# Two more merge gates computed as fills inside the RWKV part of a two-block hybrid mixer

## Chip, cores and metric

The kernel runs on one core of a Trainium2 chip. The metric is the device time of one execution in microseconds; lower is better. For a kernel the median of several runs counts.

## What is computed

The input is 256 tokens of width 2048 (x) and 256 context tokens (ctx). The first block is a hybrid mixer with four branches (a convolution, a state-space scan "SSD", a Fourier branch and an RWKV-7 scan), whose outputs are merged by gates, and then an MLP; a second block follows. The part that matters is the merge, for 256 tokens and D = 2048:

```python
def gated_merge(gate_pre, branches, w_o):
    b, l, _ = gate_pre.shape
    gates = jax.nn.sigmoid(gate_pre).reshape(b, l, N_BRANCH, D_MODEL)
    m = gates[:, :, 0] * branches[0]
    for i in range(1, N_BRANCH):
        m = m + gates[:, :, i] * branches[i]
    return m @ w_o
```

`gate_pre` is a slice of `u = h @ w_in`: 4 x 2048 columns, each a sum over 2048. It depends on h alone, so it can be computed as soon as h is there, long before the branches are done. The RWKV branch is a recurrence over tokens for 8 heads, forwards and backwards, first over the context (state only), then over the tokens (state and output).

## The kernel before

**Units and slots.** Weights come in units of 1024 KB (128 input features on the partitions, 16 such tiles kt, 128 output columns) through a ring of four slots. SP issues every fetch: the fetch of unit u waits until unit u - 4 is used up (`w_used`). Queues run in order, so whatever SP waits for holds up all that stands behind it.

**Gates.** The merge goes over 8 pairs of output tiles (p = 0..7), with four gates each (b = 0..3), one per branch: 32 gates. A gate takes two units (o = 0, 1) and fills one PSUM bank of 128 x 512.
- Gates b = 0 and 2 of every pair, 16 in all (`FILLS`), are computed early, as *fills*: `fill(pe, n)` (line 953) issues the next n plain fp32 matmuls of 128x128 by 128x256 (line 966) of one running list of 32 per gate, in places chosen by hand, where TensorE would wait. The matmul is recorded as two instructions. The first three gates are fills of the SSD part, the other 13 of the RWKV part.
- ACT turns a finished bank into a gate with a sigmoid (`fill_gates`, line 975, recorded at line 980), at one place in each round: `fills_by(r)` (line 971) works out from `FILL_PREP`, `FILL_ROUND` and `FILL_EARLY` how many gates are complete there. SP then stores it in DRAM (`keep_gate`, line 984, recorded at 986). In `RwScan.sync` the fetch of gate k is followed by the storing of gate k - 2.
- Gates b = 1 and 3 are computed in the merge itself, in `Merge.tensor`, with weights and h split in high and low parts: three fp32r products per tile (lines 2067 to 2069), 96 a gate. ACT rounds each unit (`round_unit`, line 2310), DVE takes the difference (`rest_unit`, line 2315), three and two units ahead.

**Preparation of the RWKV part** (`RwIn`, lines 1229 to 1386). TensorE projects 14 tiles (line 535). ACT copies each into a padded buffer (1290, 1294), DVE shifts and mixes them (1350 to 1354). Then TensorE turns the values (line 1246, "turned values", four banks), multiplies the learning-rate part (1251, waits for `al_ready`, which DVE raises at line 1358 after the last shift), the output gate (1258), makes 12 fills, the sums for the key norm (1265), 12 fills, and the bonus sums (1272). ACT makes sigmoids (1308), copies (1311), squares (1316) and roots (1323). DVE ends with four reciprocals (1375) and the bonus (1382), and raises `prep_ready` (1386).

**The rounds** (`RwScan`, from line 1493). Eight rounds: for each of four head pairs j first the context (half = 1), then the tokens (half = 0). Before them TensorE computes the first decays (`decays(0)`, line 1512) and 24 fills. A round on TensorE: 7 fills; products of the scaled keys (1531), after DVE's line 1806; turned tiles (1572, 1573), 4 fills; five levels of the triangular inverse (1542, 1556) with fills between; turned left side (1600); *masked products* (`products`, 1531: one pair of banks in a context round, three in a token round), which DVE masks at line 1846; the next round's decays (1512); inverse right side (1616), after the mask, copied by ACT at line 1768; 6 or 3 fills; the inverse applied (1542, `tav`), after that copy; 3 fills; the state updates (1636 to 1643); in a token round also 1656 and then the *output* `y_in` (1669, 1672); 3 fills; the chunk states (1695) and in a token round 1709. In ACT's queue between the levels and line 1768 stand the decay gates of the next round (table load and two sigmoids, 1724) and the kept gates (980). There are 47 fills in a context round and 44 in a token round.

**The merge** (`Merge`, from line 2047). SP fetches, for each pair, the four units, then the branch weights `bo_u[p]` (2304 KB, one buffer, after the products of pair p - 1), then, after the sums of pair p - 1 (`merged`), the two kept gates (256 KB each). TensorE: gate, gate, then 36 matmuls of branch outputs by branch weights (line 2086). DVE: four times a unit's difference and one column of the second block's modulation (rows of 1024 KB, fetched by POOL, 389), then the products with the gates (2162 to 2168).

## Time and profile before

| | us |
|---|---|
| median of 3 runs (lowest to highest) | 3455.66 (3454.62 to 3462.45) |
| the profiled execution's own time | 3459.0 |
| its span in the profile | 3457.3 |
| TensorE busy / DVE / ACT | 3283.2 / 2166.8 / 1183.7 |
| preparation of the RWKV part after its projections, from and to | 711 to 765 |
| eight rounds, from and to | 765 to 1164 |
| merge, from and to | 1172 to about 1482 |

The profile is of one execution. TensorE's matmuls overlap, and their ends are modelled: the time that a row of equal instructions takes is read from start to start. A timeline row gives start, duration, engine, line, instruction, operands and count, and in brackets the idle time before it with what ended it.

### The profile page before, as it was taken

Reading aid. Unit: us, or ns where it says so; the run is one execution under the profiler, and the core shown is the slowest. Engines: PE = TensorE matmul, PEld = TensorE weight load, DVE = VectorE, ACT = ScalarE, POOL = GpSimd, SP = SyncE. Lnnn points to the kernel's source line nnn. Section 1 sums busy time; section 2 is a strip of 40 time slices with the busy share of each in tenths; the row PEclk is TensorE's granted clock in tenths of the full one; section 3 lists DMA queues with packets and bytes.
Section 4 is the critical chain, followed back from the end, with each engine's and each line's share of the span. In section 5 each row is a group of like instructions: output and inputs, shape, how many; then the busy total and the mean of one; then the engine's idle time right before and its main releaser. Section 6 shows DMA issues by size and latency. Waiting matters only on the chain.

```text
span 3457.3 us, 57768 instructions
## 1 busy us (share of the span) xinstructions
PE 3283.2 (95%) x23026; PEld 2687.1 (78%) x23026; DVE 2166.8 (63%) x3283; ACT 1183.7 (34%) x1550; POOL 188.6 (5%) x298
## 2 busy tenths in 40 slices
PE   6899989989998899998999999998999999999998
PEld 3674676457777799987888888886888788888887
DVE  2185654663333565667777777787656767667767
ACT  1212021022222321234434343444544543444344
POOL 0000000111222100000000000000000000000000
PEclk9999999999999999999999999999999999999999
DMA  9864624722112477754676767673444556656654
GB/s 364 327 230 170 264 105 158 292 92 84 71 44 84 190 309 307 292 185 158 246 263 235 272 229 282 231 268 122 158 153 176 172 193 234 235 187 229 233 177 151
DMA packets 99280, 706.33 MB, mean 204 GB/s; under 512 B 11008, under 2 KB 11008, under 8 KB 17920
## 3 DMA queue, kind: packets, MB, share of 16 engines
q1 hardware_dynamic: 74880, 523.27, 41.5%
q0 software_dynamic: 23184, 169.88, 13.3%
q10 hardware_dynamic: 1008, 10.23, 0.7%
q8 instruction: 152, 2.49, 0.3%
q14 instruction: 56, 0.46, 0.0%
HBM read 697.05 MB, written 6.29 MB: 203 GB/s over the span
## 4 chain that ended last, share of the span: by engine, by line
PE 76%; DVE 9%; issue 6%; ACT 4%; DMA 3%; DVEq 0%; ACTq 0%; SPq 0%; POOLq 0%
PE ps L2352 25%; PE ps L2351 13%; PE ps L535 10%; PE ps L966 6%; PE ps L2086 3%; ACT rows_parts L2310 3%; PE ps L355 2%; PE ps L1542 2%; PE ps L2348 2%; PE ps L2068 2%; PE ps L2067 2%; PE ps L2069 2%; PE ps L1556 1%; DVE work L2196 1%; DMA ring<-in_conv_u 1%
## 5 line engine op out<-in xcount | busy, mean ns | idle before, releaser
L2352 PE MATMUL ps<-hT_parts,rows_parts 128*128 128x512 f32 x3210 | 1129.8, 394 | 0.0
L2351 PE MATMUL ps<-hT_parts,ring_parts 128*128 128x256 f32 x3210 | 900.7, 281 | 2.0 <-DVE hT_parts L2324 2.0
L2315 DVE TENSOR_TENSOR ring_parts<-ring,rows_parts 128x2048 fp32r<-128x2048 f32 (+1 forms) x340 | 769.6, 2264 | 208.6 <-ACT rows_parts L2310 207.2
L2310 ACT ACTIVATE rows_parts<-ring 128x2048 fp32r<-128x2048 f32 (+1 forms) x340 | 643.8, 1895 | 414.9 <-DMA ring<-in_mlp_u 167.6
L2352 PEld LDWEIGHTS ps<-hT_parts,rows_parts 128*128 128x128 f32 x3210 | 603.5, 188 | 125.6
L2351 PEld LDWEIGHTS ps<-hT_parts,ring_parts 128*128 128x128 f32 x3210 | 608.0, 189 | 12.9 <-DVE hT_parts L2324 3.2
L2352 PE MATMUL ps<-work_parts,rows_parts 128*128 128x512 f32 x1616 | 573.3, 396 | 0.0
L2351 PE MATMUL ps<-work_parts,ring_parts 128*128 128x256 f32 x1616 | 453.1, 280 | 4.6 <-DVE work_parts L2540 4.6
L535 PE MATMUL ps<-hT,ring 128*128 128x512 f32 (+1 forms) x1088 | 374.2, 505 | 7.4 <-ACT work L1294 4.3
L2352 PEld LDWEIGHTS ps<-work_parts,rows_parts 128*128 128x128 f32 x1616 | 303.6, 188 | 68.2
L535 PEld LDWEIGHTS ps<-hT,ring 128*128 128x128 f32 x1088 | 206.0, 190 | 173.8 <-issue 162.1
L2351 PEld LDWEIGHTS ps<-work_parts,ring_parts 128*128 128x128 f32 x1616 | 304.3, 188 | 11.0 <-DVE work_parts L2540 5.9
L966 PE MATMUL ps<-hT,ring 128*128 128x256 f32 x1024 | 271.5, 403 | 3.1 <-DVEq L1386 3.1
L2395 ACT ACTIVATE work<-ps 128x256 f32<-128x256 f32 (+1 forms) x220 | 83.2, 378 | 465.0 <-PE ps L2352 457.2
L2400 DVE TENSOR_TENSOR work<-work,ps 128x256 f32<-128x256 f32 (+1 forms) x220 | 92.1, 418 | 197.1 <-ACT work L2395 176.4
L966 PEld LDWEIGHTS ps<-hT,ring 128*128 128x128 f32 x1024 | 187.2, 195 | 33.4 <-DVEq L1386 3.5
L389 DVE CUSTOM_DVE_ANT_0 rows<-rows 128x2048 f32<-128x2048 f32 x64 | 146.4, 2288 | 37.7 <-DMA rows<-in_mod_r 37.6
L2196 DVE CUSTOM_DVE_ANT_0 work<-work,K 128x2048 f32<-128x2048 f32 x64 | 146.2, 2285 | 4.1 <-DMA work<-in_ada_r 4.0
L2069 PE MATMUL ps<-hT_parts,ring_parts 128*128 128x256 f32 x512 | 145.1, 283 | 0.0
L2086 PE MATMUL ps<-work 128*128 128x256 f32 x576 | 125.6, 379 | 0.0
L1826 DVE TENSOR_TENSOR work<-work,ps 128x64 f32<-128x64 f32 x288 | 42.2, 213 | 133.1 <-PE ps L1556 132.0
L2086 PEld LDWEIGHTS ps<-work 128*128 128x128 f32 x576 | 108.8, 190 | 14.5
(444 smaller groups left out, 3784.3 us busy)
## 6 DMA issues: line engine op xcount, KB each, us to landing
ring<-in_mlp_u SPq DMA_DIRECT2D x128, 1024.0 KB, 4.9
ring<-in_ffn_u SPq DMA_DIRECT2D x88, 1024.0 KB, 4.8
rows<-in_mod_r POOLq DMA_DIRECT2D x64, 1024.0 KB, 5.2
ring<-in_gate_u SPq DMA_DIRECT2D x64, 1024.0 KB, 6.7
work<-in_ada_r POOLq DMA_DIRECT2D x64, 1024.0 KB, 5.1
ring<-in_in_u SPq DMA_DIRECT2D x36, 1024.0 KB, 4.8
ring<-in_mod_u SPq DMA_DIRECT2D x32, 1024.0 KB, 7.7
rows<-in_ada_r POOLq DMA_DIRECT2D x32, 1024.0 KB, 7.6
```

What stands on the lines that cost most here:

```text
L389: dve.tensor_tensor_reduce(rows_buf[:, j, :], rows_buf[:, j, :], conditioning, 1.0, 0.0, ALU.mult, ALU.add, g_acc[:, j:j + 1]).then_inc(ro ...
L535: mm = pe.matmul(outs[o], wtile(u + o, kt), rhs(kt), start=kt == 0, stop=kt == KT - 1)
L966: mm = pe.matmul(ps[:, use_fill[k][0], o * T:(o + 1) * T], wtile(u, kt), main_rhs(kt), start=kt == 0, stop=kt == KT - 1)
L2069: mm = pe.matmul(out, low, h_high[:, kt, :], start=False, stop=kt == KT - 1)
L2086: mm = pe.matmul(ps[:, 3 + b, o * T:(o + 1) * T], bo_buf[:, at + kt, o * P:(o + 1) * P], src[:, kt, :], start=kt == 0, stop=kt == kts - 1)
L2196: dve.tensor_tensor_reduce(late_row, late_row, c2_row, 1.0, 0.0, ALU.mult, ALU.add, acc).then_inc(late_free, 1)
L2310: act.activation(unit_high(u)[:, 0:size], slot(u)[:, 0:size], ACT.Copy).then_inc(hi_done, 1)
L2315: dve.tensor_tensor(ring_parts[:, u % SLOTS, 0:size], slot(u)[:, 0:size], unit_high(u)[:, 0:size].bitcast(F32), ALU.subtract)\
L2351: pe.matmul(ps[:, b, low_half], low, top(kt), start=False, stop=False)
L2352: mm = pe.matmul(ps[:, b, :], high, both(kt), start=False, stop=kt == kts - 1)
L2395: act.activation(dst, ps[:, b:b + 1, half], ACT.Copy).then_inc(half_out, 1)
L2400: dve.tensor_tensor(dst, dst, ps[:, b:b + 1, half], ALU.add).then_inc(bk.free[b], 1)
```

## The change

Gate 1 of pair 3 and gate 1 of pair 5 become fills too, and are kept in DRAM like the others: 18 fills instead of 16 (15 in the RWKV part), 14 gates in the merge instead of 16. The 64 more fill matmuls stand: 12 before the turned values, 8 more after the first decays (24 becomes 32), 3 after the first masked products in all rounds, 2 before the inverse is applied and 3 before the output in token rounds. ACT reads gate 3 before the first decay exponentials instead of in round 0, and the number of gates read in each round follows the new counts. In the merge, pairs 3 and 5 have one computed gate and three kept ones; DVE makes the same four columns a pair; SP fetches each pair's units up to four past its first one. The host lays the weight columns out in the new order.

```diff
--- before.py
+++ after.py
@@ -58,6 +58,9 @@
 UNIT = KT * P
 PARTS2 = (16, 16, 12)
 BO_K = CT + ST + FT + RT
+MORE_KEPT = ((3, 1), (5, 1))
+KEPT_GATES = [(p, b) for p in range(KT // 2) for b in (0, 2)] + list(MORE_KEPT)
+MERGE_GATES = [(p, b) for p in range(KT // 2) for b in (1, 3) if (p, b) not in MORE_KEPT]
 
 
 
@@ -932,8 +935,9 @@
         ssq = w(S0 + 5632, ST * T, a=ST)
 
         PAIRS2 = KT // 2
-        FILLS, SSD_FILLS = 2 * PAIRS2, 3
-        FILL_PREP, FILL_ROUND, FILL_EARLY = 48, 44, 31
+        FILLS, SSD_FILLS = len(KEPT_GATES), 3
+        FILL_PREP, FILL_HALF, FILL_FULL, FILL_EARLY = 68, 50, 52, 31
+        FILL_FIRST = 36
         seg_ssd_fill = segment(2 * SSD_FILLS)
         use_fill = [bk.take(k) for k in range(SSD_FILLS)]
         fill_gate, fill_stored = sem("fill_gate"), [sem(f"fill_stored{n}") for n in range(2)]
@@ -970,7 +974,10 @@
 
         def fills_by(r):
 
-            return min(FILLS - 1, SSD_FILLS + (FILL_PREP + FILL_ROUND * r + FILL_EARLY) // (2 * KT)) if r >= 0 else SSD_FILLS
+            if r < 0:
+                return SSD_FILLS + FILL_FIRST // (2 * KT)
+            before = FILL_PREP + r // 2 * (FILL_HALF + FILL_FULL) + r % 2 * FILL_HALF
+            return min(FILLS - 1, SSD_FILLS + (before + FILL_EARLY) // (2 * KT))
 
         def fill_gates(act, first, last):
             for k in range(first, last):
@@ -1239,6 +1246,7 @@
                     both = n >= 2
                     outs = [ps[:, 0, :], ps[:, 1, :]] if both else pair(n % 2)
                     gemm_pair(pe, seg_rw + 2 * n, both_rhs if both else main_rhs, outs, rw_uses[n])
+                fill(pe, 12)
                 for a in range(NT):
                     pe.wait_ge(shifted, 3 * RT)
                     acquire(pe, use_vt[a])
@@ -1513,7 +1521,7 @@
                                   lora_t[d * LORA:(d + 1) * LORA, half * T:(half + 1) * T], start=True, stop=True).then_inc(bk.full[use[0]], 1)
 
                 decays(0)
-                fill(pe, 24)
+                fill(pe, 32)
                 pe.wait_ge(prep_ready, 1)
                 for r, (j, half) in enumerate(ROUNDS):
                     u = rounds[r]
@@ -1604,6 +1612,8 @@
                             pe.wait_ge(rsem["r_ready"][d], j + 1)
                     for n, (left, right) in enumerate(((3, 0),) if half else ((3, 0), (1, 4), (3, 4))):
                         products([u["nt"][h][n] for h in range(2)], left, right)
+                        if n == 0:
+                            fill(pe, 3)
                     if r + 1 < len(ROUNDS):
                         decays(r + 1)
                     for h in range(2):
@@ -1616,6 +1626,8 @@
                                 mm = pe.matmul(ps[across(odd), use[0], blk(i)], BIG[h][0][rows, blk(i)], v_of(h, a, rows), start=True, stop=True)
                         mm.then_inc(bk.full[use[0]], 1)
                     fill(pe, 6 if half else 3)
+                    if not half:
+                        fill(pe, 2)
                     evacuated(pe, u["at"])
                     for h in range(2):
                         evacuated(pe, u["nv"][h])
@@ -1657,6 +1669,7 @@
                                                start=True, stop=True)
                                 if i == len(UNITS) - 1 and h == 1:
                                     mm.then_inc(bk.full[u["rh"][odd][0]], 1)
+                        fill(pe, 3)
                         use = u["y_in"]
                         acquire(pe, use)
                         for a in range(TT):
@@ -1730,6 +1743,7 @@
                         act.activation(dec_mem(2, d), dec_mem(1, d), ACT.Exp, scale=DECAY).then_inc(rsem["dec_exp"][d], 1)
 
                 decay_gates(0)
+                fill_gates(act, SSD_FILLS, fills_by(-1))
                 decay_exps(0)
                 act.wait_ge(prep_ready, 1)
                 for r, (j, half) in enumerate(ROUNDS):
@@ -1983,8 +1997,8 @@
                         .then_inc(yt_aff, 1)
 
 
-        seg_merge = segment(4 * PAIRS2)
-        MERGE_END = seg_merge + 4 * PAIRS2
+        seg_merge = segment(2 * len(MERGE_GATES))
+        MERGE_END = seg_merge + 2 * len(MERGE_GATES)
         MERGE_ROWS = 4 * PAIRS2
         bo_buf = w(W0, BO_K * 2 * P, k=BO_K)
         gates = w(W0 + BO_K * 2 * P, 8 * T, b=4)
@@ -1992,7 +2006,7 @@
         m_all = w(M0, KT * T, a=KT)
         H0 = M0 + KT * T
         assert H0 + UNIT <= WORK
-        use_gate = [bk.take(b, PAIRS2) for b in range(2)]
+        use_gate = [bk.take(n, sum(b == g for _, b in MERGE_GATES)) for n, g in enumerate((1, 3))]
         use_bo = [bk.take(3 + b, PAIRS2) for b in range(4)]
         bo_ready = sem("bo_ready")
         merged = sem("merged")
@@ -2000,14 +2014,24 @@
         h_hi, h_split, x_again = sem("h_hi"), sem("h_split"), sem("x_again")
 
         GATED = (1, 3)
-        KEPT = (0, 2)
         kept_in = sem("kept_in")
 
+        def gated(p):
+
+            return [n for n, b in enumerate(GATED) if (p, b) in MERGE_GATES]
+
+        def kept(p):
+
+            return [b for b in range(4) if (p, b) in KEPT_GATES]
+
         def merge_unit(p, n, o=0):
-            return seg_merge + 4 * p + 2 * n + o
+            return seg_merge + 2 * MERGE_GATES.index((p, GATED[n])) + o
+
+        def merge_units(p):
+            return [merge_unit(p, n, o) for n in gated(p) for o in range(2)]
 
         def gate_use(p, n):
-            return n, use_gate[n][1] + p
+            return n, use_gate[n][1] + sum((q, GATED[n]) in MERGE_GATES for q in range(p))
 
         def unit_high(u):
 
@@ -2025,13 +2049,13 @@
 
         class Merge:
             def sync(sp):
+                fetched = seg_merge
                 for p in range(PAIRS2):
-                    for n in range(2):
-                        for o in range(2):
-                            u = merge_unit(p, n, o)
-                            sp.wait_ge(w_used, u - SLOTS + 1)
-                            sp.dma_start(slot(u), gate_u[2 * FILLS + u - seg_merge]).then_inc(w_ready[u % SLOTS], 16)
-                        if p == 0 and n == 0:
+                    for u in range(fetched, min(merge_unit(p, gated(p)[0]) + SLOTS, MERGE_END)):
+                        sp.wait_ge(w_used, u - SLOTS + 1)
+                        sp.dma_start(slot(u), gate_u[2 * FILLS + u - seg_merge]).then_inc(w_ready[u % SLOTS], 16)
+                        fetched = u + 1
+                        if u == seg_merge + 1:
                             keep_gate(sp, FILLS - 2)
                     if p == 0:
                         keep_gate(sp, FILLS - 1)
@@ -2046,13 +2070,13 @@
                     else:
                         for n in range(2):
                             sp.wait_ge(fill_stored[n], 8 * FILLS)
-                    for n, b in enumerate(KEPT):
-                        sp.dma_start(gates[:, b, :], gate_kept[2 * p + n]).then_inc(kept_in, 16)
+                    for b in kept(p):
+                        sp.dma_start(gates[:, b, :], gate_kept[KEPT_GATES.index((p, b))]).then_inc(kept_in, 16)
 
             def tensor(pe, own):
                 fill(pe, 2 * FILLS * KT - fills_read[0])
                 for p in range(PAIRS2):
-                    for n in range(2):
+                    for n in gated(p):
                         use = gate_use(p, n)
                         acquire(pe, use)
                         for o in range(2):
@@ -2100,7 +2124,8 @@
                 fill_gates(act, FILLS - 1, FILLS)
                 for p in range(PAIRS2):
                     act.wait_ge(merged, p)
-                    for n, b in enumerate(GATED):
+                    for n in gated(p):
+                        b = GATED[n]
                         for o in range(2):
                             u = merge_unit(p, n, o)
                             if u == seg_merge + 1:
@@ -2138,18 +2163,20 @@
                 RwOut.vector_scaled(dve, own)
                 m_pairs = m_all.rearrange("p (j o) t -> p j o t", o=2)
                 for p in range(PAIRS2):
-                    for n in range(4):
-                        u = seg_merge + 4 * p + n + AHEAD_DVE
+                    units = merge_units(p)
+                    for n, u in enumerate(units):
+                        u += AHEAD_DVE
                         if u == seg_merge + 1 + AHEAD_ACT:
                             RwOut.vector_out(dve, own)
                         rest_unit(dve, u)
-                        at = 4 * p + n
-                        for i in (at,) if p else () if n < 2 else (2 * n - 4, 2 * n - 3):
+                        late = n if p else n - 2
+                        each = 4 // (len(units) if p else 2)
+                        for i in range(4 * p + late * each, 4 * p + (late + 1) * each) if late >= 0 else ():
                             if i == 0:
                                 dve.wait_ge(c2_moved, 1)
                             column(dve, adaT, vec("ada_b"), c2_row, ADA0 + i, i)
-                    dve.wait_ge(kept_in, 32 * p + 32)
-                    for n in range(2):
+                    dve.wait_ge(kept_in, 16 * sum(len(kept(q)) for q in range(p + 1)))
+                    for n in gated(p):
                         evacuated(dve, gate_use(p, n))
                     if p == PAIRS2 - 1:
                         unit_done(dve, MERGE_END - 1)
@@ -3468,7 +3495,7 @@
 
     bo = np.concatenate([i[k][0] for k in ("conv_out", "ssd_out", "fourier_out", "rwkv_out")], 0)
     gates = w_in[:, gt:].reshape(D, 4, KT // 2, 2 * P)
-    gates = np.concatenate([gates[:, n::2].transpose(0, 2, 1, 3).reshape(D, -1) for n in range(2)], 1)
+    gates = np.concatenate([gates[:, b, p] for p, b in KEPT_GATES + MERGE_GATES], 1)
     ffn = np.stack([i["w_ffn_gate_2"][0].reshape(D, KF2, P), i["w_ffn_up_2"][0].reshape(D, KF2, P)], 2).reshape(D, -1)
 
     up, down = i["mlp_up"][0], i["mlp_down"][0]
```

## Rows read from the trace of the kernel before

**Rows 1.** The page: span, and busy time of each engine

```profile
span 3457.3 us, 57768 instructions
...
PE 3283.2 (95%) x23026; PEld 2687.1 (78%) x23026; DVE 2166.8 (63%) x3283; ACT 1183.7 (34%) x1550; POOL 188.6 (5%) x298
```

**Rows 2.** Stretches: length, busy PE, PEld, DVE, ACT, POOL; granted clock, DMA, GB/s

```profile
712.00:772.00 60.00, 51.18 (x275) 37.19 (x273) 40.37 (x55) 22.60 (x43) 5.20 (x7) 0.86 0.15 53
...
823.00:878.00 55.00, 49.03 (x1021) 39.47 (x1013) 19.77 (x80) 13.50 (x31) 10.52 (x15) 0.94 0.13 45
...
1237.00:1275.00 38.00, 38.00 (x264) 36.19 (x263) 25.17 (x27) 10.27 (x8) 2.64 (x5) 1.00 0.80 306
...
718.30:725.40 7.10, 7.10 (x8) 2.49 (x8) 5.12 (x10) 2.06 (x3) 0.00 (x0) 0.50 0.01 2
```

**Rows 3.** Timeline of TensorE in the preparation of the RWKV part

```profile
718.30 7.19 PE L1251 MATMUL ps<-work 64*128 64x512 f32 x8 [5.41 <-DVEq L1358]
725.42 3.78 PE L1258 MATMUL ps<-work 128*128 128x256 f32 x8
728.99 5.90 PE L966 MATMUL ps<-hT,ring 128*128 128x256 f32 x24
734.73 3.79 PE L1265 MATMUL ps<-work,K 128*128 128x512 f32 x8
738.35 5.34 PE L966 MATMUL ps<-hT,ring 128*128 128x256 f32 x24
743.53 1.89 PE L1272 MATMUL ps<-work,K 128*128 128x256 f32 x8
...
759.75 4.98 PE L966 MATMUL ps<-hT,ring 128*128 128x256 f32 x14 [3.14 <-DVEq L1386]
```

**Rows 4.** Timeline of DVE in the same stretch

```profile
739.37 3.35 DVE L1375 RECIPROCAL work<-work 128x512 f32<-128x512 f32 x1 [10.20 <-ACT work L1323]
...
764.47 0.42 DVE L1806 TENSOR_TENSOR work<-rows,work 128x256 f32<-128x256 f32 x1
```

**Rows 5.** Waits, 772 to 1164: who waited for whom, total us, times, longest

```profile
PE ps L1531 <- DVE work L1846: 5.3, 4, 1.3
PE ps L1669 <- issue: 5.3, 3, 3.4
...
PE ps L1616 <- DVE work L1846: 4.3, 4, 1.1
...
PE ps L1542 <- issue: 2.9, 3, 1.5
PE ps L1672 <- issue: 2.8, 1, 2.8
```

**Rows 6.** Timeline of TensorE around the output of the first two token rounds

```profile
853.45 0.26 PE L1672 MATMUL ps<-work 64*64 64x64 f32 x1 [2.79 <-issue]
...
855.88 2.93 PE L966 MATMUL ps<-hT,ring 128*128 128x256 f32 x6
858.74 0.69 PE L1695 MATMUL ps<-work 64*64 64x64 f32 x8
...
953.89 0.22 PE L1672 MATMUL ps<-work 64*64 64x64 f32 x1
...
955.33 1.56 PE L966 MATMUL ps<-hT,ring 128*128 128x256 f32 x6
956.82 0.45 PE L1695 MATMUL ps<-work 64*64 64x64 f32 x8
```

**Rows 7.** Timeline of ACT in round 0

```profile
795.91 0.66 ACT L1768 ACTIVATE work<-ps 128x256 f32<-128x256 f32 x2
```

**Rows 8.** The chain that ended last, in order of time: start, us, what

```profile
1236.28 15.54 PE ps L2086 x72
1274.69 15.54 PE ps L2086 x72
```

**Rows 9.** The eight fetches of branch weights, their time to landing

```profile
DMA to landing us min/median/max: 8.4/9.0/10.5
```

**Rows 10.** DMA issues from 772 to 1164: KB each, median us to landing

```profile
ring<-in_gate_u SPq DMA_DIRECT2D x23, 1024.0 KB, 5.8
```

## The prediction

> **What bounds the kernel now.** I read the page first [rows 1]: TensorE is busy 3283.2 of 3457.3 us, so a change counts by what it adds to or takes from TensorE's own stream, and by the 174 us in which that stream stands still. Then the busy time by stretches [rows 2]: in a merge pair (1237 to 1275) TensorE is busy the whole 38.00 us at clock 1.00, DVE 25.17, ACT 10.27, DMA at 0.80. In the preparation (712 to 772) and in a closing round (823 to 878) TensorE has 9 and 6 us of holes and a mean granted clock of 0.86 and 0.94. Then TensorE's timeline there [rows 3, 5, 6] and the engines it waits for [rows 4, 7]. "Issue" in a row is idle time for which the profile shows no semaphore.
>
> **Removed.** Two gates (branch 1 of pairs 3 and 5) leave the merge. The products with the branch outputs (L2086) start at 1236.28 and again at 1274.69, and take 15.54 [rows 8]. So a pair lasts 38.41 us, of which 38.41 - 15.54 = 22.87 are its two gates: 11.43 each. TensorE has no hole there [rows 2], so two gates give 2 x 11.43 = **-22.9 us**. Their four weight units, roundings (ACT) and differences (DVE) go too, off the path.
>
> **Added.** The same two gates as plain fp32 fills: 64 matmuls, each two instructions at L966. At full clock 24 instructions go from 738.35 to 743.53 [rows 3], 216 ns each, so one fill is 0.432 us and 64 are 27.6 us. At full price the change would lose 4.8. All hangs on where they stand.
>
> *Preparation, 12 fills before the turned values (5.2 us) and 8 more after the first decays (3.5 us).* TensorE turns the values at 711 and then stands 5.41 us until VectorE has shifted the last tile (L1358) at 718.30 [rows 3]. That release hangs on DVE and ACT, not on TensorE, so 5.2 us fit in front; the values are then turned from about 716.3 to 718.1, with nothing late. After that hole the trace shows granted clock 0.50, that is 1.2 GHz instead of 2.4, from 718.3 to 725.4 [rows 2]: L1251 takes 7.12 us to the start of L1258 [rows 3]. Without the hole the engine goes on at 2.4 GHz: L1251 3.56 (-3.6), L1258 3.57 to the start of the fills, now 1.7 by 8 x 216 ns (-1.8), and the 24 fill instructions 5.74 instead of 5.18 (-0.6). Sum -6.0. It passes on, since DVE's reciprocals (L1375) at 739.37 waited 10.20 us for ACT's roots [rows 4], and these for TensorE's L1265. I expect ACT's sigmoids at L1308 to keep up with products that come twice as fast; rival 2 is the case that they don't. The 0.1 us that ACT's copies of the values come later I take off: **-5.9**. From L1375 on DVE sets the pace until prep_ready at 759.7; the 8 fills (3.5) stand in the 3.14 us hole at 759.75 [rows 3], whose wait I expect at about 0, as TensorE itself is 5.9 earlier too. ACT's extra sigmoid, of fill 3, lies in its wait for DVE's first sums. Round 0 still starts when DVE's L1806 is through (764.47 + 0.42 [rows 4]), 5.9 earlier. The fills after 759.75 took 4.98 for 14 instructions at the low clock; running faster they only wait for L1806.
>
> *Masked products, 3 fills (1.3 us) in each of 8 rounds.* In the four context rounds TensorE waits 4.3 us in all at L1616, in the four others 5.3 at L1531 [rows 5], each time for DVE's masking. The fills come ahead of the next round's decays, so in a context round ACT's table load, decay gates and kept gates start 1.3 us later and the copies of L1768, at 795.91 + 0.38 [rows 7], come at about 797.6 where TensorE begins L1542 at about that time today. That is 0.4 instead of 0.2 beyond cover in three of them. Sum: 4 x 1.3 - 4.3 + 0.45 = +1.35; in the others 5.2 - 5.3 = 0.
>
> *Before the turned inverse times values (L1542), 2 fills in four rounds (3.45 us).* The holes there are 2.9 in three rounds, the longest 1.5 [rows 5], so 0.7 + 0.7 + 0.86 are covered and the last round has none: **+1.15**.
>
> *Before the output (L1669), 3 fills in four rounds (5.2 us).* Here TensorE stands 5.3 + 2.8 = 8.1 us in four holes, 3.4 and 2.8 and two of about 1, marked "issue" [rows 5]. They fall at different matmuls of the same line, so no semaphore of that line makes them. They come behind the longest run of 64-column products without a fill in it (L1636 to L1672). I take them for instructions that arrive late; the trace does not prove this. If so, 1.3 us of slow matmuls ahead of it shortens each hole by up to 1.3: 1.3 + 1.3 + 0.9 + 1.0 = -4.5. After the 2.79 us hole the rest runs at the low clock: 853.45 to 858.74 is 5.29 us, where after a hole of 1 us 953.89 to 956.82 is 2.93, and six fill instructions last 2.93 instead of 1.56 [rows 6]. A hole of 1.5 us is followed by full clock elsewhere (L1531's 1.33), so that loss of 2.4 goes. The 3.4 hole shrinks to 2.1, between 1.5 and 2.79; both ends are equally near, and I take the loss, some 3.0, as kept. Together 5.2 - 4.5 - 2.4 = **-1.7**. Bounds: +5.2 (no hole shrinks) and -8.3 (all holes and both clock losses gone: 5.2 - 8.1 - 5.4).
> The Trainium skill, page "Runtime: NRT & Kernel Launch", section "Instruction fetch mechanics", says that instructions are refilled in 16 KiB blocks and that this is mostly hidden behind the rate at which instructions issue. By that rule the holes are no late instructions and the fills cost their +5.2; the row of 8.1 us speaks against it, without settling it.
>
> *Queues.* Each fetch on SP stands behind the storing of an earlier gate. The tightest is now fill 13: it waits for gate 10, read by ACT in round 4, and is needed at the 320th fill of this part, the last but two of that round. In times of round 0 that is SP at about 797 and TensorE at about 807, for a landing of 5.8 us [rows 10]: 4 us to spare, price 0. In the merge, the branch weights of pairs 3 and 5 must land in the 11.43 us of one gate instead of 22.87; they take 8.4 to 10.5 [rows 9]. One more gate of 256 KB beside them, by 2304 KB in 9.0 us, is 1.0 us at worst: 11.5, nothing to 0.1 late. DVE is busy 25.17 us of 38 in a pair of today [rows 2], and loses two of its four differences. Price 0, bound +5 each.
>
> **Sum.** -22.9 - 5.9 + 1.35 + 0 + 1.15 - 1.7 = **-28.0 us**. The profiled execution took 3459.0 (span 3457.3) and goes to 3431.0; it lies 3.3 above the median of the three runs, 3455.66, which goes to **3427.7**.
>
> **Rivals.**
> 1. *The output's holes stay*: +5.2 in place of -1.7, the sum -21.1: 3434.6. For it: the holes' cause is unproven. Against: they sit where instructions are shortest. The page named above would give just this. 0.15.
> 2. *The preparation gains nothing*: the hole is filled but the copies of the values come late, or the clock stays low, so +0.3 for the 8 fills in place of -5.9: 3433.9. For it: ACT does sigmoids and copies one behind the other. Against: clock 0.50 begins exactly behind the hole. 0.10.
> 3. *The merge becomes bound by transfers* in its two short pairs: two weight units, the branch weights, three gates and four rows of the modulation matrix are 9216 KB or 9.4 MB, in 27 us 350 GB/s, above the 306 of [rows 2]. At 306 a pair needs 31 us: +4 each, 3435.5. 0.06.
> 4. *Nothing is covered*: -22.9 + 27.6 = +4.8, 3460.4, which is no change. Against: 29 us of holes stand in [rows 3, 5], before any low clock is counted. 0.04.
> 5. *Slower: a weight unit arrives late in each round*, because its fetch is queued behind a gate's store that waits for ACT, which the new fills push back. A hole of 2.8 us and its clock loss of 2.4 are 5.2, in 8 rounds 41.8: -28.0 + 41.8 = +13.8, 3469.5. It decides once a landing takes over 10 us. Against: 5.8. 0.03.
> That the gates are not moved at all I leave out: the lists are 18 and 14 gates by count.
> The forecast itself has 0.62.
>
> **The numbers.** About 0.3%, 10.4 us, is what a measurement can tell. Faster: the forecast and rivals 1 to 3, 0.93; same: rival 4 and a mixture, 0.04; slower 0.03. Low end: all holes and both clock losses gone, 6.6 below, with 2 for the rest: 3419. High end: rivals 1 and 2 together, 3440.8: 3441.
>
> **What would show it.** TensorE's hole before L1251 under 0.5 us and L1251 at 427 ns a start at clock 1.00; prep_ready about 6 us earlier; no wait at L1616's and L1531's places; the holes before and in the output under 1.6 us but one; pairs 3 and 5 of the merge at 27 us with TensorE unbroken; the merge starting 5 us sooner than before (-5.9 - 1.7 + 1.35 + 1.15). Wrong if the merge starts no earlier, or if L2086 waits in pairs 3 and 5.

## Result, and the profile after

| | before | after |
|---|---|---|
| median (lowest to highest) | 3456.89 (3454.62 to 3462.45), 4 runs | 3425.14 (3423.72 to 3434.82), 4 runs |
| ratio, with its 95% interval | | 0.9911 [0.9892, 0.993] |
| the profiled execution's own time | 3459.0 | 3434.82 |

The change takes 31.75 us, 0.9%. Forecast were 28.0 and a time of 3427.7: the direction, the range and the size are right. Two parts of the sum are not, and their errors cancel in large part. The profiles were cut into five stages behind a common start; the stages' lengths are differences of start times in the timeline.

| stage, us | before | before again | after | after again |
|---|---|---|---|---|
| start of the learning-rate product (1251, now 1259) | 718.30 | 717.73 | 728.08 | 725.11 |
| from there to round 0 | 46.70 | 46.18 | 40.91 | 40.91 |
| round 0 to the first gate product of the merge | 406.95 | 400.72 | 410.51 | 408.82 |
| first gate product to first branch product | 25.85 | 25.36 | 25.55 | 24.86 |
| first to last branch product | 284.1 | 284.1 | 261.2 | 261.2 |
| last branch product to the end | 1975.41 | 1976.40 | 1966.85 | 1966.09 |

"Again" are two more executions, from the experiments below. The first row holds work that the change doesn't touch; over all profiles of this study it lies between 716.4 and 728.1 in no order. It is what scatters, so single executions can't be compared by their ends, but by their stages they can.

The page of the kernel after (answers to rows 1):

```profile
span 3433.1 us, 57659 instructions
...
PE 3284.7 (96%) x22962; PEld 2689.7 (78%) x22962; DVE 2160.1 (63%) x3279; ACT 1177.9 (34%) x1546; POOL 188.6 (5%) x298
```

TensorE is as busy as before (3283.2 in [rows 1]), in a span 24.2 us shorter: the same work with fewer holes. DVE and ACT have four instructions of work fewer each. That small number becomes important below.

TensorE's timeline in the preparation, after (answers to rows 3):

```profile
720.77 5.34 PE L970 MATMUL ps<-hT,ring 128*128 128x256 f32 x24
725.95 1.91 PE L1254 MATMUL ps<-K,work 128*128 128x128 f32 x16
728.08 3.70 PE L1259 MATMUL ps<-work 64*128 64x512 f32 x8 [0.22 <-DVEq L1366]
731.71 1.99 PE L1266 MATMUL ps<-work 128*128 128x256 f32 x8
733.54 5.34 PE L970 MATMUL ps<-hT,ring 128*128 128x256 f32 x24
738.72 3.79 PE L1273 MATMUL ps<-work,K 128*128 128x512 f32 x8
...
749.98 17.10 PE L970 MATMUL ps<-hT,ring 128*128 128x256 f32 x78
768.99 1.16 PE L1539 MATMUL ps<-work 64*64 64x64 f32 x64 [1.91 <-issue]
```

The hole of 5.41 us is down to 0.22, and the product behind it takes 3.63 us (728.08 to 731.71) instead of 7.12. The windows of the same trace, with the columns of rows 2, give the clock:

```profile
728.10:735.00 6.90, 6.90 (x23) 4.33 (x24) 5.75 (x11) 5.16 (x10) 0.00 (x0) 1.00 0.01 2
...
1281.93:1308.83 26.90, 26.90 (x170) 25.04 (x169) 18.69 (x19) 4.39 (x4) 1.58 (x3) 1.00 0.70 268
...
1308.83:1347.24 38.41, 38.41 (x266) 36.55 (x265) 23.49 (x25) 8.46 (x6) 2.11 (x4) 1.00 0.89 353
```

The first: granted clock 1.00 where it was 0.50. The second is pair 3, with one computed gate: TensorE is busy through all 26.90 us. The third is pair 4: the queues move 353 GB/s, with TensorE as busy. The chain that ended last has the branch products:

```profile
1281.93 15.54 PE ps L2110 x72
...
1308.83 15.54 PE ps L2110 x72
...
1347.24 15.54 PE ps L2110 x72
...
1374.29 15.54 PE ps L2110 x72
```

26.90, 38.41, 27.05: two pairs lost 11.5 and 11.4 us, and 22.9 together.

TensorE's waits from 766 to 1185, after (answers to rows 5; line 1682 is the old 1669, 1539 the old 1531, 1550 the old 1542, 1668 the old 1656, 1652 the old 1640):

```profile
PE ps L2091 <- DVE hT_parts L2160: 7.5, 1, 7.5
PE ps L1682 <- issue: 3.4, 2, 1.9
PE ps L1539 <- issue: 3.3, 4, 1.9
...
PE ps L1668 <- DVE work L1871: 1.9, 1, 1.9
PE ps L1652 <- issue: 1.5, 1, 1.5
...
PE ps L1550 <- ACT work L1782: 0.6, 3, 0.2
PE ps L1550 <- issue: 0.5, 1, 0.5
```

The waits for DVE's masks (5.3 and 4.3 in [rows 5]) are gone. The holes in the runs of 64-column products, 8.1 before, are 6.8 now (3.4 + 1.9 + 1.5), at other lines. The 1.9 is put down to VectorE, but TensorE's two semaphore instructions there begin only at 856.16 and take 0.05 us each, so they found nothing to wait for: it is counted with the others. And the wait of 7.5 at the head of the merge, which was there before as well, still is.

Last, the part behind the merge, which the edit doesn't touch and which the prediction didn't name, is 8.6 us shorter. VectorE's rows for the line at the head of the MLP loop, before and then after (the loop makes four turns, each a quarter of the hidden width):

```profile
L2400 DVE TENSOR_TENSOR work<-work,ps x220: 407/420/424, 1490.2 to 3375.3; 128x256 f32<-128x256 f32 x94, 128x256 f32 x16
...
  issue: 20.4, 3
```

```profile
L2427 DVE TENSOR_TENSOR work<-work,ps x220: 409/420/424, 1473.9 to 3351.0; 128x256 f32<-128x256 f32 x94, 128x256 f32 x16
...
  issue: 11.9, 3
```

The same instruction stands still three times, at the three turns of the loop, for no semaphore: 20.4 us in all before, 11.9 after. The difference, 8.5, is the stage's.

### The profile page after: what moved, and what is told of

It is laid out like the page before. It is cut to its first block, busy times and chain, and to the rows that moved or that the text cites. A ratio compares the mean times of both kernels' runs of the same rounds, so it can differ in the third digit from the quotient of the medians.

```text
span 3433.1 us, 57659 instructions
## 1 busy us (share of the span) xinstructions
PE 3284.7 (96%) x22962; PEld 2689.7 (78%) x22962; DVE 2160.1 (63%) x3279; ACT 1177.9 (34%) x1546; POOL 188.6 (5%) x298
## 4 chain that ended last, share of the span: by engine, by line
PE 81%; DVE 7%; issue 5%; ACT 4%; DMA 3%; DVEq 0%; ACTq 0%; POOLq 0%; SPq 0%
PE ps L2379 27%; PE ps L2378 14%; PE ps L538 10%; PE ps L970 6%; PE ps L2110 4%; PE ps L358 2%; ACT rows_parts L2337 2%; PE ps L2375 2%; PE ps L1550 2%; PE ps L2092 2%; PE ps L2091 2%; PE ps L2093 2%; PE ps L1564 1%; DMA ring<-in_conv_u 1%; DVE work L2223 1%
## 5 line engine op out<-in xcount | busy, mean ns | idle before, releaser
L2378 PE MATMUL ps<-hT_parts,ring_parts 128*128 128x256 f32 x3210 | 900.9, 281 | 1.6 <-DVE hT_parts L2351 1.6
L538 PEld LDWEIGHTS ps<-hT,ring 128*128 128x128 f32 x1088 | 206.0, 190 | 173.8 <-issue 162.1
L970 PE MATMUL ps<-hT,ring 128*128 128x256 f32 x1152 | 297.2, 396 | 0.0
L970 PEld LDWEIGHTS ps<-hT,ring 128*128 128x128 f32 x1152 | 207.1, 191 | 32.5 <-issue 2.7
L2093 PE MATMUL ps<-hT_parts,ring_parts 128*128 128x256 f32 x448 | 127.0, 283 | 0.0
```

Source lines behind the costliest of these rows:

```text
L538: mm = pe.matmul(outs[o], wtile(u + o, kt), rhs(kt), start=kt == 0, stop=kt == KT - 1)
L970: mm = pe.matmul(ps[:, use_fill[k][0], o * T:(o + 1) * T], wtile(u, kt), main_rhs(kt), start=kt == 0, stop=kt == KT - 1)
L2093: mm = pe.matmul(out, low, h_high[:, kt, :], start=False, stop=kt == KT - 1)
L2378: pe.matmul(ps[:, b, low_half], low, top(kt), start=False, stop=False)
```

## Experiments

Three questions stood open. Is the gain of the preparation due to the fills ahead of the turned values? Do fills ahead of the output shorten its holes, or do the holes go by where the instructions lie (theory P of the expectations)? And where do the 9 us behind the merge come from: VectorE's code lying four instructions earlier (theory A1), or ACT's?

### How much of a profile is chance

The two kernels unchanged, once more: before_again and after_again.

> The kernel before once more, for a second trace. Between the end of the merge and the end of the MLP the changed kernel's trace is 8.9 us shorter than that of before, although nothing there was edited: VectorE stands 6.3, 6.9 and 7.3 us at the turn of the MLP's loop before, 4.6, under 3.5 and 4.3 after. Theory A (the place of the code in memory sets the stall): this second trace shows 6 to 7 us again at each turn. Theory B (chance of one execution, for instance what the transfers do at that moment): the stalls come out anywhere between 3 and 7.5. Both: the holes before the output in the token rounds (2.8, 0.8, 3.4, 1.1) repeat within 0.3 if they are fixed by the code, and scatter if by chance.

> The changed kernel once more, against before in three rounds. Its profiled execution had a start 9.8 us longer than that of before, in stages not edited; without it its own time would be 3425, as in the other runs. Expected: ratio 0.991, some 31 us less. By Theory A 25 of these come from the edited stages and 6 to 9 from the loop of the MLP in every run; by Theory B only about 25 to 28 us as a mean, and the MLP's stalls are other than 4.6, under 3.5, 4.3.

after_again took 3426.42, before beside it 3460.44 (7 runs, 3448.45 to 3465.4): ratio 0.9913 [0.9882, 0.9944]. Stages as in the table. VectorE's stops at the turns of the loop repeat: 7.0, 7.1 and 7.0 us in before_again (6.3, 6.9, 7.3 before), 4.1, 4.5 and 3.3 in after_again. So do before's holes around the output: 2.82, 0.50, 3.17 and 1.10 against 2.79, 0.78, 3.44 and 1.10. Both speak for the code's place. Rounds 1 and 5 of the kernel before took 56.29 and 57.86 us in the first profile, 53.49 and 54.78 now, with holes that are nearly as long (3.2 and 2.8). TensorE's row behind the hole in round 1 of before_again, and the window around it, columns as in rows 2:

```profile
852.44 0.21 PE L1672 MATMUL ps<-work 64*64 64x64 f32 x1 [2.82 <-issue]
```

```profile
851.00:860.00 9.00, 6.80 (x112) 5.22 (x111) 1.42 (x6) 3.00 (x6) 0.00 (x0) 1.00 0.01 2
```

Clock 1.00 behind a hole of 2.82 us, where the first profile had half of it for 5.29 us behind one of 2.79 [rows 6]. In the two padded versions of before, below, rounds 1 and 5 took 56.1 to 56.3 us, so the loss comes in three of four executions and is no fixed part of the kernel. It isn't bound to long holes either: in after_dve_pad4, below, whose TensorE code is that of after, the clock is at 0.50 for 3.4 us behind holes of 1.91 and 1.94 us that left it at 1.00 in after.

### The first 12 fills behind the hole again (first_fills_late)

```diff
-                fill(pe, 12)
                 for a in range(NT):
                     pe.wait_ge(shifted, 3 * RT)
...
-                fill(pe, 32)
+                fill(pe, 44)
                 pe.wait_ge(prep_ready, 1)
```

> The changed kernel with the 12 fills taken from before the turned values and put behind the first decays (44 fills there instead of 32). My theory: the hole of 5.4 us before L1259 comes back, the clock falls to 0.50 behind it and costs 6.0 us, and the 5.2 us of fills are no longer covered: TensorE then reaches round 0 by 19.0 us of fills and 3.0 more after the decays, so that round 0 starts about 9 us later than in the changed kernel (50 instead of 40.9 us after L1259's start). Time +9, about 3434. Rival (the fills in the hole keep no clock up, VectorE's chain sets the time anyway): the start of round 0 moves by at most 3 us.

TensorE's timeline of first_fills_late:

```profile
723.15 7.19 PE L1258 MATMUL ps<-work 64*128 64x512 f32 x8 [5.40 <-DVEq L1365]
730.27 3.78 PE L1265 MATMUL ps<-work 128*128 128x256 f32 x8
```

The hole is back, and so is the product at half clock. Round 0 begins 50.01 us after the learning-rate product, against 40.91: +9.1. The key sums (line 1272) begin at 739.70, 16.55 us behind that product instead of 10.64, so the low clock costs 5.9; the 12 fills cost 5.2, less the 1.9 us hole ahead of round 0, which is gone. The time is 3431.67 (3429.96 to 3439.85) against 3426.42 (3422.59 to 3431.44), +5.3 with ranges that overlap; ratio 0.9927 [0.9899, 0.9956]. The stage shows the effect, the medians only its sign. The forecast for this place is shown by removal.

### Output fills moved into the wait at the merge (output_fills_to_merge)

```diff
-        FILL_PREP, FILL_HALF, FILL_FULL, FILL_EARLY = 68, 50, 52, 31
+        FILL_PREP, FILL_HALF, FILL_FULL, FILL_EARLY = 68, 50, 49, 31
...
-                        fill(pe, 3)
                         use = u["y_in"]
...
             def scalar(act, own):
+                fill_gates(act, fills_by(len(ROUNDS) - 1), FILLS - 1)
```

The 12 fills then stand at the end of the list, behind the last round, ahead of the merge's 7.5 us wait.

> The changed kernel with the 3 fills before the output taken out of the four token rounds and put at the end, so that 16 instead of 4 fills stand before the merge, where TensorE stands 7.5 us for VectorE's split of h. Covered there: 12 x 0.43 = 5.2 us, and some of the 2.5 us of low clock behind that hole. Theory L (the holes in the token rounds are instructions that come late, and slow matmuls ahead of them shorten each by their own length): each hole grows by up to 1.3 us, two of them pass 2.7 us and bring back the low clock at 2.4 to 3 us each; together +8 to +10, so the gain at the merge is eaten: 0 to +2 us. Theory P (the holes hang on where the 16 KB blocks of code end, not on what stands before): their sum stays 5 to 8 us by other places, and the time falls by about 6 to 8 us, to about 3418.

TensorE's waits of output_fills_to_merge from 740 to 1200:

```profile
PE ps L2090 <- DVE hT_parts L2160: 2.3, 1, 2.3
PE ps L1681 <- issue: 2.1, 2, 1.7
PE ps L1668 <- DVE work L1870: 1.3, 1, 1.3
...
PE ps L970 <- issue: 0.7, 1, 0.7
```

Without fills ahead of them the holes are 2.1 and 1.3, 3.4 in all, and 0.7 more in round 4's fills; with them 6.8 (5.1 in after_again). Theory L asked for longer holes without the fills, and they are shorter. But the edit also moves the code of TensorE, so the two aren't separated by this run alone. The clock fell here behind the hole of 1.7 us. The 12 fills now cover 5.2 of the 7.5 us wait. Rounds 402.59 (after_again 408.82), and from the first gate to the first branch product 23.62 (24.86). Time 3417.88 (3412.61 to 3422.38), 8.5 less than after_again; ratio to before 0.9893 [0.9864, 0.9923].

### The round's fills back at its head (round_fills_at_head)

```diff
-                    fill(pe, 7)
+                    fill(pe, 10 if half else 15)
...
-                        if n == 0:
-                            fill(pe, 3)
...
-                    if not half:
-                        fill(pe, 2)
...
-                        fill(pe, 3)
                         use = u["y_in"]
```

> The changed kernel with the 44 new fills of the rounds all at the head of each round (10 instead of 7 in context rounds, 15 in token rounds), where TensorE waits at most 0.7 us, and none at the masked products, the inverse and the output. The rounds of before took 400.7 us to the first gate product with no low clock in them (second trace of before). My theory: the holes at L1616, L1531 and L1542 come back, 12.5 us in all, the fills cost their 19.0, and the rounds take 400.7 + 19.0 = 419.7 less 0 to 2 us, against 408.8 and 410.5 in the two traces of the change: time +8 to +11. Rival (the places cover nothing, a fill costs the same anywhere): rounds 409 to 411 and the time unchanged.

TensorE's waits of round_fills_at_head, same stretch:

```profile
PE ps L1539 <- DVE work L1855: 5.3, 4, 1.3
PE ps L1624 <- DVE work L1855: 4.3, 4, 1.1
PE ps L1677 <- issue: 4.0, 2, 2.9
...
PE ps L1550 <- issue: 2.9, 3, 1.5
PE ps L1648 <- issue: 2.1, 1, 2.1
PE ps L1680 <- issue: 1.7, 1, 1.7
```

The waits of the kernel before return to the tenth (5.3, 4.3, 2.9 in [rows 5]), and the holes among the 64-column products are 7.8, with the clock at 0.50 for 3.4 us behind three of them (1.7, 2.1 and 2.9). The rounds take 422.17 us, 11.7 to 13.4 more than in the two profiles of after. Time 3436.39, against 3427.11 of after_dve_pad4 on the same chip: +9.3; ratio 0.9942 [0.9921, 0.9962]. It is the place of the fills in the round that pays, and the masked products are the larger part of it (9.6 us of the 12.5 in waits). These longer holes, 7.8 against 6.8 and 5.1, and their low clock are in the 11.7 to 13.4 too, so that isn't the price of the place alone.

### More instructions on TensorE ahead of the rounds (after_pe_pad128)

```diff
                 fill(pe, 32)
+                for n in range(128):
+                    pe.wait_ge(al_ready, 1)
                 pe.wait_ge(prep_ready, 1)
```

The waits are on a semaphore long since up; nothing is computed otherwise. They became 64 instructions (57723 in the page against 57659), half of what the expectation counts with.

> The changed kernel with 128 more waits, long fulfilled, on TensorE ahead of the wait for prep_ready: its code in the rounds moves by half a block, and nothing else changes there. Theory P (the holes without a releaser in the rounds come where blocks of code end): the holes, so far 0.97 to 1.94 us after 87 and 292 us, 1.5 after 240 and 1.7 to 1.9 after 392 us from round 0, come at other places with other lengths, none, or up to 3.5 us. Theory L (they come wherever the short products run longest, whatever the position): one hole in each token round's output again, within 0.5 us of those lengths. Cost of the waits themselves: 0 to 3 us before round 0.

TensorE's waits of after_pe_pad128, same stretch:

```profile
PE ps L1684 <- issue: 3.5, 2, 2.2
...
PE ps L970 <- issue: 3.0, 1, 3.0
PE ps L1670 <- issue: 2.6, 1, 2.6
...
PE ps L1687 <- issue: 0.7, 1, 0.7
```

Line 1684 is after's 1682 and 1670 its 1668. The hole of 3.0 us ahead of round 0, which begins 2.9 us later (43.81 instead of 40.91), is no moved hole but the padding itself, from `--source L1526`:

```profile
L1526 PEldq EVENT_SEMAPHORE  x63: 51/51/51, 752.7 to 759.4; - x63
```

63 of the 64 waits are recorded, one every 0.11 us, and the fills behind them begin at 759.65. In the rounds four executions of after's TensorE code (after, after_again, after_dve_pad4, after_dve_pad8) agree: a hole at line 1668 in round 1 (1.0 to 1.9 us), one at line 1682 in round 5 (1.2 to 1.4) and one at 1682 in round 7 (1.7 to 1.9); that of 1.5 at L1652 comes in two of the four. With the padding round 1 has 1.3 at the old 1682, round 3 a new one of 0.7 at L1687, round 5 still one at the old 1682, now 2.2, and round 7 has 2.6 at the old 1668. Holes that move when only the number of instructions ahead of them changes aren't made by the lines at which they stand. This speaks for P, with one execution of the padded kernel. That the engine waits there for its own instructions is the simplest reading; no row names it.

Over all profiles there is no relation between fills ahead of the output and the holes: without them 6.9 to 8.1 (before's code), 7.8 (round_fills_at_head), 3.4 (output_fills_to_merge) and 5.3 (fewer_products_fills), with them 4.6 to 6.8 (after's code), 6.3 (first_fills_late) and 6.8 here.

### Padding on VectorE and ACT

Four kernels, each with waits that are already fulfilled put at one point, behind the merge's products on VectorE or at its head on ACT.

```diff
 after_dve_pad4, after_dve_pad8 (n + 1 for n < 4; n % 4 + 1 for n < 8)
+                for n in range(8):
+                    dve.wait_ge(merged, n % 4 + 1)
                 dve.wait_ge(merged, PAIRS2)
 before_dve_pad128
+                for n in range(128):
+                    dve.wait_ge(merged, n % 8 + 1)
                 dve.wait_ge(merged, PAIRS2)
 before_act_pad20
+                for n in range(20):
+                    act.wait_ge(h_hi, n % 4 + 1)
                 fill_gates(act, FILLS - 1, FILLS)
```

> The changed kernel with four more waits, on a semaphore long at its value, on VectorE at the end of the merge: it executed four operations less there than before. Two traces of before show VectorE standing 6.3 to 7.3 us at each of the three turns of the MLP's loop, four traces of kernels with the change 4.5 us or less, and 1975.4 and 1976.4 us against 1965.9 to 1966.9 from the last product of the merge to the end. Theory A1 (the position of VectorE's code to the instruction): the stalls return to 6.3 to 7.3 and the rest of the kernel takes some 9 us longer, time about 3434. Theory A2 (position too, but only where a whole block moves): stalls stay at 4, the rest at 1966. Theory C (a cause outside VectorE's code): the same as A2.

> The kernel before with 128 such waits on VectorE at the end of the merge, half a block of 16 KB. Theories A1 and A2: the stalls at the turns of the MLP's loop move out of 6.3 to 7.3 us, probably to 3 to 5, and the rest of the kernel after the merge comes to 1966 to 1970 us plus up to 3 us for the waits themselves. Theory C: the stalls stay at 6.3 to 7.3 and the rest at 1975 to 1979.

> The four waits of after_dve_pad4 came to only two more executed instructions on VectorE (2402 before the first turn of the MLP's loop, against 2400 in the changed kernel and 2404 in before); eight waits should bring exactly the 2404 of before. Theory A1 (VectorE's position to the instruction): quarters of the MLP take 183.6 us as in before instead of 180.3 to 181.0, and the stretch from the merge's last product to the end 1975 instead of 1966. Theory A2 (VectorE's position matters only by larger shifts; 128 waits took the quarter of before to 181.3) or theory D (another engine's code, TensorE's or ACT's): quarters stay at 180 to 181 and the stretch at 1966 to 1968.

> The kernel before with 20 more fulfilled waits on ACT at the head of the merge, which should come to 10 executed instructions, as many as the change added on ACT ahead of the MLP. Theory D-ACT (ACT's position sets how long VectorE stands at the turn of the MLP's loop): quarters of 180 to 181.5 us instead of 183.6, the stretch after the merge 1966 to 1968. All others: 183.3 to 183.7 and 1975 to 1977.

The pages of after_dve_pad4 and of after_dve_pad8 give 57661 and 57663 instructions. So four waits became two instructions (after has 57659), and after_dve_pad4 tested half a step: its 3427.11 us, with the stops of after, say nothing for or against A1. The count of VectorE's instructions executed up to the branch at the first loop turn, taken from the trace, waits and register instructions included:

| kernel | VectorE instructions | loop turns, us | last branch product to the end |
|---|---|---|---|
| before | 2404 | 183.6, 183.4, 183.7 | 1975.41 |
| after | 2400 | 181.0, 179.4, 180.6 | 1966.85 |
| after_dve_pad4 | 2402 | 180.8, 180.8, 180.4 | 1967.66 |
| after_dve_pad8 | 2404 | 183.1, 183.5, 183.1 | 1975.18 |
| before_dve_pad128 | 2468 | 181.4, 181.2, 181.4 | 1977.65 |
| before_act_pad20 | 2404 | 183.8, 183.6, 183.5 | 1977.5 |

With four instructions put back, and nothing else changed, the 8.3 us are back. (The loop's own body isn't quite that of before: a turn has 324 instructions in the kernels with the change and 322 in before, the two more being register instructions. So 2404 puts the branch where it was, and the head of the loop two instructions ahead of that.) VectorE's timeline at the second turn of after_dve_pad8:

```profile
1947.62 0.42 DVE L2429 TENSOR_TENSOR work<-work,ps 128x256 f32<-128x256 f32 x1 [4.09 <-issue]
1950.97 0.43 DVE L2567 SCALAR_TENSOR_TENSOR work<-work 128x256 f32<-128x256 f32 x1 [2.94 <-issue]
```

and at the first turn of after:

```profile
1776.19 0.42 DVE L2427 TENSOR_TENSOR work<-work,ps 128x256 f32<-128x256 f32 x1 [4.55 <-issue]
1776.64 0.42 DVE L2565 SCALAR_TENSOR_TENSOR work<-work 128x256 f32<-128x256 f32 x1
```

With the padding a second stop comes one instruction later: 4.09 + 2.94 = 7.0, as long as the single one of before (6.3 to 7.3). That single one is two as well. In the trace of before, the branch ends at 1785.15 and one operation starts at once; then the next instruction, a register instruction of L2529, comes only at 1789.50, and the one after it, L2400, at 1793.82: two stops of 4.3 us. In after there is one, from the branch's end at 1769.28 to 1776.08. Over the three turns the line views give 12.3 us at L2429 and 8.8 at L2567, 21.1 against before's 20.4 and after's 11.9. So theory A1 holds: what the part behind the merge gained is a matter of where VectorE's code lies. before_act_pad20, whose ACT executes 986 instructions up to there (987 in after, 976 in before), keeps the long turns: ACT's code is not it. Nor is TensorE's: after_pe_pad128 takes 1965.93 for this part. before_dve_pad128 shows the same from the other side: its turns are short (14.0 us of stops at them instead of 20.4). Its time doesn't show it, because of what stands just behind the merge:

```profile
1492.06 0.43 DVE L2324 CAST hT_parts<-work 128x512 fp32r<-128x512 f32 x1 [6.12 <-issue]
```

```profile
L2170 DVEq EVENT_SEMAPHORE  x63: 21/50/556, 1485.3 to 1491.8; - x63
```

These 6.1 us are the padding: VectorE executes its waits one every 0.10 us, and line 2324 comes when they are through. Without them the part behind the merge would take 1971.5 instead of 1976.4, an estimate: 1977.65 - 6.1.

### Fewer fills at the masked products, none at the output (fewer_products_fills)

```diff
-        FILL_PREP, FILL_HALF, FILL_FULL, FILL_EARLY = 68, 50, 52, 31
+        FILL_PREP, FILL_HALF, FILL_FULL, FILL_EARLY = 72, 47, 49, 31
...
-            before = FILL_PREP + r // 2 * (FILL_HALF + FILL_FULL) + r % 2 * FILL_HALF
+            before = FILL_PREP + (r + 1) // 2 * FILL_HALF + r // 2 * FILL_FULL + (3 if r else 0)
...
-                fill(pe, 32)
+                fill(pe, 36)
...
-                        if n == 0:
+                        if n == 0 and (not half or r == 0):
                             fill(pe, 3)
...
-                        fill(pe, 3)
                         use = u["y_in"]
...
             def scalar(act, own):
+                fill_gates(act, fills_by(len(ROUNDS) - 1), FILLS - 1)
```

Four more fills go into the hole ahead of round 0, and three context rounds lose theirs: nine fills leave the rounds, and the rest stand behind the last one.

> output_fills_to_merge, and beyond it 9 fills taken from the masked products of three context rounds (where a group of 3 costs 0.7 us more than it covers, 46.99 against 46.26), 4 of them put into the 1.9 us hole before round 0 and 5 into the 2.3 us left before the merge. My theory: three context rounds go from 47.0 to 46.3, the hole before round 0 from 1.9 to 0.2, that before the merge from 2.3 to 0.2: -2.1 us against output_fills_to_merge, about 3416 where that had 3418, and 9 to 11 below the changed kernel. Rival (the rounds' holes without releaser move again with the code): the sum of the rounds changes by 2 to 4 us either way, whatever the fills.

TensorE's waits of fewer_products_fills from 740 to 1200:

```profile
PE ps L1626 <- DVE work L1859: 3.2, 3, 1.1
...
PE ps L1684 <- issue: 1.9, 1, 1.9
PE ps L1652 <- issue: 1.8, 1, 1.8
...
PE ps L2090 <- DVE hT_parts L2160: 1.4, 1, 1.4
...
PE ps L1655 <- issue: 1.1, 1, 1.1
```

The hole ahead of round 0 is filled (0.18 left), the wait at the merge is 1.4; the three context rounds have their 1.1 us wait for the mask back, and yet take 46.28, 46.49 and 49.68 (the last with the 1.8 hole and the clock at 0.50 for 3.4 us behind it) against 46.94, 48.65 and 46.63 in after. Rounds 403.63, about output_fills_to_merge's 402.59: moving the product fills brought nothing that can be told. Time 3414.72 (3410.03 to 3420.73), before beside it 3459.2: ratio 0.9867 [0.9849, 0.9886], the best of the study, 13 us beyond the change as made, with an interval clear of its [0.9892, 0.993], though not quite of after_again's [0.9882, 0.9944].

## Why the prediction was right, point by point

It was right in the merge and in the preparation, which are its two large terms. In the rounds it was wrong by 4.7 us, and what made up for that lies behind the merge, where it expected nothing. Its own sign of being wrong came: the merge was to start 5 us sooner, and "wrong if the merge starts no earlier". From the learning-rate product to the first gate product it is 450.8 us before and 450.7 after, by the means below.

The measured column compares means: over the four profiles with before's rounds (before, before_again and its two padded versions) and the four with after's (after, after_again, after_dve_pad4 and after_dve_pad8). The row behind the merge leaves out before_dve_pad128 and after_dve_pad8, whose padding changes that stage.

| step | forecast | measured | from, to |
|---|---|---|---|
| merge | -22.9 | -22.9 | 284.1 to 261.2 |
| preparation | -5.9 | -5.6 | 46.52 to 40.91 |
| rounds | +0.8 | +5.5 | 404.28 to 409.80 |
| behind the merge | 0 | -9.6 | 1976.4 to 1966.9 |
| sum | -28.0 | -32.6 | medians: -31.75 |

**Merge and queues: right.** A gate is worth 11.43, and the branch products of pairs 3 and 5 never waited: the queues moved 268 GB/s in pair 3 and 353 in pair 4, more than the 306 by which rival 3 was priced. That rival falls, and 5 with it: no weight unit came late in a round.

**Preparation: right in the mechanism and in the size.** All three parts are in the rows: hole 0.22, the product 3.63, the output gate 1.83 to the start of the fills. (The 427 ns a start among the signs don't fit the sum's own 3.56 us for eight, which are 445; measured are 454.) The forecast that ACT keeps up is borne out, since the key sums start at 10.64 instead of 16.43 and the gain arrives at round 0. Ahead of round 0 a hole of 1.91 us marked "issue" is left. TensorE waits there for another engine, as the step said of DVE's line 1806: the trace of after has a semaphore instruction of TensorE from 763.93 to 768.93, and the VectorE operation of the old line 1806 ends at 768.88. So there was room for four more fills, and with them (fewer_products_fills) round 0 starts no later (40.91). Rival 2 falls.

**Masked products and turned inverse (+1.35, 0 and +1.15, 2.5 in all): right in the mechanism, mis-sized.** The waits of 12.5 us went, as said. But three fills between 64-row products cost more than their 1.30 us. TensorE's timeline of after in round 0:

```profile
795.73 1.56 PE L970 MATMUL ps<-hT,ring 128*128 128x256 f32 x6
797.22 0.70 PE L1520 MATMUL ps<-work 64*128 64x256 f32 x4
```

From start to start it is 1.49. [rows 6] had it already: 955.33 to 956.82 is 1.49 for six such instructions. The prediction took 216 ns each from a run of 24, and so left out 0.2 a group, in eight groups here and four ahead of the output: 2.4 us. With it this step is 8 x 1.49 + 3.45 - 12.5 + 1.1 (the waits at 1550) = +4.0.

**Output: the failed step.** "I take them for instructions that arrive late ... 1.3 us of slow matmuls ahead of it shortens each hole by up to 1.3 ... -4.5." The holes did get shorter, from a mean of 7.5 us (8.1, 7.6, 6.9, 7.6) to 5.3 (6.8, 5.1, 4.7, 4.6), but nothing shows that the fills did it: with these away they are 3.4. The padded run speaks for the position of the code, and then it could have come out the other way. The clock loss, "-2.4", is about what the means leave: rounds +5.5, less 4.0, less 4 x 1.49 - 2.2 = 3.8 for fills and holes, is -2.3. But it is a chance event: before's executions have it three times in four, and of the four with after's rounds one (after_dve_pad4). So this step cost some +1.5 instead of bringing 1.7, and rival 1 (+5.2) was nearer for the fills and the holes alone, which is what the page "Runtime: NRT & Kernel Launch" of the Trainium skill, section "Instruction fetch mechanics", would give with its fetches mostly hidden. If these holes, 3.4 to 8.1 us of them, are fetches, which no run here settles, then "mostly hidden" doesn't hold in these rounds.

**Behind the merge: not in the prediction at all.** VectorE's four differences that leave the merge were priced at nothing ("off the path"). As work they are. As a shift of the code by 4 instructions they were worth more than the preparation: 8.3 us, shown by after_dve_pad8 in one execution, against 1965.9 to 1967.7 in the eight other profiles of kernels with the change. The two errors, +4.7 in the rounds and -9.6 here, have opposite signs, so the total came out nearer than its parts deserved. That was luck. Without it the time would have been about 3434, still in the range, and what rival 1 gives.

**Left open.** Why 2404 instructions give two stops a turn and 2400 one; why the second comes one instruction later in after_dve_pad8 than in before; whether "issue" on TensorE is its instruction fetch; and why the clock falls in one execution and not in the next behind equal holes.

## What to carry to other kernels

Put spare work where the engine waits, and remove first the wait that also costs the clock: 12 fills in front of one 5.4 us hole gained 9.1 us in their stage against the same fills behind it. Look for the longest wait that a semaphore explains before filling holes that none explains: the 12 output fills showed no gain in the rounds, and moved to the merge's wait of 7.5 us they made the time 8.5 us shorter. And cut the trace into stages: stages that the change doesn't touch may move by more than its small terms, by chance or by the code's position, and only a run with instructions put back tells which. Such padding has its own cost, here 6 to 7 us of the engine's instruction stream for 64 instructions, which must be kept apart from what it shifts.

## What the runs showed of the hardware

- VectorE stands still for 3.0 to 7.4 us at each turn of the MLP loop, behind its taken branch, marked "issue". The Trainium skill, page "Runtime: NRT & Kernel Launch", section "Instruction fetch mechanics", says that a taken branch whose target lies outside the two pages held forces a fetch before execution goes on; the place of these stops agrees with it. How long they are depends on the position of the code: 20.4 us for three turns with two stops in each, or 11.9 with one, by four instructions.
- TensorE has holes of 0.4 to 3.4 us, most of them marked "issue", in dense runs of 64-column products; 64 instructions inserted ahead moved them, in one execution.
- A hole of 2.6 to 3.4 us lowered the granted clock to 0.50 for 3.4 to 6.8 us in three executions of before's code and in a fourth not at all. Holes of 1.7 to 2.2 us did so in some executions, for 3.4 us, and not in others: 1.91 and 1.94 us in after_dve_pad4, and the same two without loss in after. The hole of 5.4 us ahead of line 1251 (1258) did it in every profile that had it (five of five).
- A group of three fp32 fills between products on 64-row tiles takes 1.49 us start to start, 0.2 more than in a long run of fills.
- Fulfilled waits on one semaphore became one instruction for two of them, and each such instruction took 0.10 us on VectorE and 0.11 on TensorE.
